# Passes outside, contraction tiles inside: a new order of the products in a split-precision block kernel

## The chip, the cores and the metric

One core of one Trainium2 chip. The metric is the device time of one execution in microseconds (us), the median of several.

## The reference

Two layers of a hybrid block on x, 1024 tokens by 1024 channels, float32. Each layer normalises x, projects it once into all branch inputs, runs four branches, gates and projects each, merges them by sigmoid gates, and adds one output projection to x.

```python
h = rms_norm(x, norm_g)
proj = h @ w_in
(q, k, v, z_a, p_in, z_b, u, v_sgu, z_c, glu_a, glu_b, z_d, merge) = jnp.split(proj, SPLIT_POINTS, axis=-1)
q = apply_rope(rms_norm(q...), cos, sin); k = apply_rope(rms_norm(k...), cos, sin)
o_a = window_attention(q, k, v, attn_sinks)
o_b = multiscale_pool(p_in, pool_mix, pool_scale)
o_c = spatial_gating(u, v_sgu, sgu_ln_g, sgu_ln_b, sgu_w, sgu_b)
o_d = conformer_conv(glu_a, glu_b, conv_w, conv_b, conv_ln_g, conv_ln_b)
...
return x + mixed @ w_out
```

## The kernel before

**Three passes.** TensorE multiplies in a rounded float32 format. To keep float32's precision, every operand is split into a rounded part ("hi": fhi, bhi, whi) and a rest (flo, blo, wlo), and a product is three matmuls, called passes here: hi by hi, lo of the data by hi of the weights, hi of the data by lo of the weights. ScalarE makes the rounded parts (a copy into the rounded format), GpSimd makes the rests of the weights (L718, a subtraction), VectorE the rests of the data (L1683, L1687).

**Stage pairs.** After the first two stages, each stage computes two tiles of 128 output channels by two halves of 512 tokens with seven products instead of eight (p1, p6, p5, p7, p2, p3, p4 in this order, a Winograd scheme): the operands are sums and differences of quarters of h (forms B11, B21, B22, B12, F5, F6, F7, F4) and of the weights (wsum). Each product has four tiles of contraction of 128 and three passes, 12 matmuls of 512 columns, written by the helper `three` (line L795). Its result goes to one of four PSUM banks a, b, c, d of `acc`; VectorE (sum_x, sum_v, sum_22, sum_12, sum_21) and ScalarE empty them. `three` runs the four tiles outside and the three passes inside, and the step begins when the rest of its weights is made (lo_made). There are four slots of split weights (SLOTS) and six of raw ones (RAWS).

**The beginning of a layer.** Stage VS (eight steps, L856 in layer 0, L885 in layer 1) has the tokens as output rows: data is the stationary operand, weights the moving one. In layer 0 the three passes are outside and four token tiles inside, and each part waits for its own hi or lo. Then `keys_values` (L906), four steps KV 0 to 3: keys and values also with tokens as rows, 256 columns (K and V side by side) for each of eight token tiles, eight contraction tiles and three passes. Slots F6 and F5 hold the first half of x until KV 1 is done, F7 and B21 the second half until KV 2 and 3. Then the stage pair Q 0 needs the forms of h: VectorE scales x by the norms (h_scale, using `spreads`, the reciprocal norms of all tokens broadcast to all partitions), forms F5, F7, F6, F4, ScalarE rounds them, VectorE subtracts for the rest. For B22, ScalarE copies the rounded part into PSUM (copy_b22), and VectorE subtracts from there (rest_b22); for the others it reads the rounded part from SBUF.

**Norms of layer 0.** ScalarE squares rows of x (row_squared, eight of them, spread over steps k = 1, 2, 3 by ROWS_AT), takes the root (rms_stage), waits for VectorE's reciprocal (norms) and stores the norms (store_norms), all at k = 3, ahead of x_rounded and the weights of k = 4. SP loads them back as `spreads`. SP's queue holds all loads of weights in order.

**Behind KV.** take_kv(0) and (1) on ScalarE copy K and V with the token's norm as scale (eight instructions each); turn_k, TensorE, turns K by eight transposes before p3 of Q 0; take_turned_k copies the result to kraw. square_a(0) and square_high(0) on ScalarE and square_low(0) on VectorE make the squares of K in two parts; head_sums(0) on TensorE (L960, L961) sums them before p5 of Q 1. inverse_root(0) on ScalarE follows. gate_stats, bn_aggr and a chain of small VectorE operations make the scaled gating values vsa; sgu_mix (L946), before p3 of Q 1, needs vsa and the root of K (qk_root).

All orders within an engine are written out by hand; engines meet at semaphores.

Of the kernel before, what the change touches and what calls it, by code (L numbers as in the profile page):

```python
# [6 lines left out]
F32 = mybir.dt.float32  # L7
# [140 lines left out]
def hybrid_block(nc, x, wstream, cols, rows, sgu_wt, pool_mix, rope, ident_in, edge_in, x_rows, out):  # L148
    ctx = ExitStack()
    with ctx:  # L150
# [80 lines left out]
        krow = place("krow", [P, TT, P], F32, at_t + 14336)  # L231
# [101 lines left out]
        b22_copied = sem("b22_copied")  # L333
        form_made = sem("form_made")
# [22 lines left out]
        kv_taken = sem("kv_taken")  # L357
        k_copied = sem("k_copied")
# [81 lines left out]

        def kv_bank(tile):

            return aux[:, tile // 4, tile % 4 * 2 * P:(tile % 4 + 1) * 2 * P]
# [341 lines left out]
        def _(pe):  # L785
            def three(dst, hi, lo, slot, kt0, first, last, cols=slice(0, HALF), resumed=False, half=None):


                for k in range(UK):
                    if half and k == UK // 2:  # L790
                        half()
                    wh = whi[:, slot, k * P:(k + 1) * P]
                    wl = wlo[:, slot, k * P:(k + 1) * P]
                    for n, (w, m) in enumerate(((wh, hi), (wh, lo), (wl, hi))):
                        mm = nc.tensor.matmul(dst, w, m[:, kt0 + k, cols], start=first and k == 0 and n == 0,  # L795
                                              stop=last and k == UK - 1 and n == 2, skip_group_check=resumed)
                return mm

            def pair(L, st, i, between=None):
                between = between or {}  # L800
                for q in PROD + (blocks(st, i) if st in MERGES else ()):
# [5 lines left out]
                    half = None  # L807
                    if (st, i) == ("Q", 0):
                        if q == "p1":
                            pe.wait_ge(form_ready, form_n(L, RESTS, "B22", 1))  # L810
                        pe.wait_ge(form_ready, form_n(L, RESTS, NEEDS[q], 0))

                        def half(q=q):
                            pe.wait_ge(form_ready, form_n(L, RESTS, NEEDS[q], 1))
                        pe.wait_ge(vs_taken, 8 * L + (6 if bank in "ab" else 8))
                    if (st, i) == ("O", 1) and q in ("p6", "p5", "p7", "p4"):
                        pe.wait_ge(mix_ready, mix_n(L, {"p6": "F6", "p5": "F5", "p7": "F7", "p4": "F4"}[q], 3))
                    pe.wait_ge(lo_made, split(L, st, i, name))
                    pe.wait_ge(taken[bank], bank_n(L, bank, (st, i), TAKEN_BEFORE[q]))
                    if (L, st, i, q) == (LAYERS - 1, "O", 3, "p4"):  # L820
# [3 lines left out]
                        for e in range(2):  # L824
                            at = slice(e * HALF // 2, (e + 1) * HALF // 2)
                            mm = three(BANK_AP["db"[e]][:, at], fhi[s], flo[s], slot, 0, e == 1, True, at,
                                       resumed=e == 0)
                            if e == 0:
                                mm.then_inc(end_done, 1)
                    elif q in PROD:  # L830
                        s = OPERAND[q]
                        mm = three(BANK_AP[bank], fhi[s], flo[s], slot, 0, q not in ("p2", "p4"), True,
                                   resumed=q in ("p2", "p4"), half=half)
                    else:
# [3 lines left out]
                        mm = three(BANK_AP[bank], bhi, blo, slot, 0, True, True, slice(t * HALF, (t + 1) * HALF))  # L838
# [53 lines left out]
            def keys_values(L):  # L892

                for k in range(4):
                    pe.wait_ge(lo_made, split(L, "KV", k))
                    slot = (L * FORMS + FORM["KV", k]) % SLOTS
                    for tile in range(TT):
                        if k == 0 and tile % 4 == 0:
                            pe.wait_ge(vs_taken, 8 * L + 2 + tile // 2)
                        for e in range(2):  # L900
                            kx = 2 * k + e
                            s = X_SLOT[kx // UK, tile // 4]
                            at = slice(tile % 4 * P, (tile % 4 + 1) * P)
                            w_at = slice(e * 2 * P, (e + 1) * 2 * P)
                            for m, (h, w) in enumerate(((fhi, whi), (flo, whi), (fhi, wlo))):
                                mm = nc.tensor.matmul(kv_bank(tile), h[s][:, kx % UK, at], w[:, slot, w_at],  # L906
                                                      start=kx == 0 and m == 0 and tile % 2 == 0,
# [202 lines left out]
        def _(act):  # L1110
# [339 lines left out]
            for k in range(1, KT):  # L1450
# [7 lines left out]
                for t in ROWS_AT[k]:  # L1458
                    row_squared(t)
# [1103 lines left out]
```

## Time and profile before

| | us |
|---|---|
| median of 3 runs (lowest, highest) | 2037.42 (2036.91, 2037.66) |
| the profiled execution | 2038.11 |
| its span, first to last instruction | 2036.2 |
| TensorE busy | 2031.4 |
| VectorE busy | 1347.7 |
| GpSimd busy | 1308.2 |
| ScalarE busy | 883.8 |

The granted clock of TensorE is 1.0 of full speed over the span. Busy time counts overlapping matmuls once; how long one takes is read from the distance of their starts, since each is shown with its own latency.

### The profile page before, as it was taken

How to read it: one execution, taken by the hardware profiler on the slowest of the kernel's cores; microseconds unless marked ns; L12 is line 12 of the kernel's file. 1: busy time of each engine (PE TensorE's matmuls, PEld its weight loads, DVE VectorE, ACT ScalarE, POOL GpSimd, SP SyncE). 2: the span in 40 equal slices, each digit the busy share in tenths (PEclk: the TensorE clock that was granted, in tenths of full speed). 3: DMA queues.
4: the chain of work that ended last, by engine and by line, in shares of the span. 5: the costliest groups of instructions: out<-in, count | busy, mean ns of one | idle time of the engine just before them, and what ended most of it. 6: DMA issues, size and time to landing. Idle time of an engine off the chain costs nothing.

```text
span 2036.2 us, 27175 instructions
## 1 busy us (share of the span) xinstructions
PE 2031.4 (100%) x9592; PEld 1690.7 (83%) x9592; DVE 1347.7 (66%) x1625; ACT 883.8 (43%) x1653; POOL 1308.2 (64%) x980
## 2 busy tenths in 40 slices
PE   9999999999999999999999999999999999999999
PEld 7988888888888888888888888888888888888887
DVE  5986543888878645338869764438888786453384
ACT  6655644343233334324647455443432343443242
POOL 2767555776669667554727675467766797675545
PEclk9999999999999999999999999999999999999999
DMA  7133323313431343313431332223135213434142
GB/s 277 38 94 86 93 92 112 96 52 84 90 72 52 83 83 79 138 52 114 145 90 37 104 94 94 99 89 94 57 78 97 65 57 81 91 73 145 42 135 104
DMA packets 122758, 186.13 MB, mean 91 GB/s; under 512 B 30976, under 2 KB 40320, under 8 KB 122624
## 3 DMA queue, kind: packets, MB, share of 16 engines
q1 hardware_dynamic: 105040, 155.14, 24.8%
q0 software_dynamic: 9216, 16.78, 6.1%
q10 hardware_dynamic: 8368, 12.47, 1.9%
q8 instruction: 78, 1.28, 0.3%
q14 instruction: 56, 0.46, 0.1%
HBM read 141.34 MB, written 41.95 MB: 90 GB/s over the span
## 4 chain that ended last, share of the span: by engine, by line
PE 97%; DVE 1%; DMA 1%; SPq 0%; ACT 0%; issue 0%; DVEq 0%; POOL 0%; ACTq 0%; POOLq 0%
PE acc L795 88%; PE aux L906 2%; PE acc L885 1%; PE aux L885 1%; PE aux L978 1%; PE acc L999 1%; PE aux L946 1%; PE aux L1014 1%; PE aux L986 1%; PE acc L856 1%; PE aux L856 1%; DVE flo L1683 0%; DMA x<-x 0%; DMA xrow<-x_rows 0%; PE aux L960 0%
## 5 line engine op out<-in xcount | busy, mean ns | idle before, releaser
L795 PE MATMUL acc<-fhi,whi 128*128 128x512 f32 x2140 | 834.9, 390 | 0.2 <-DVE x L1680 0.2
L718 POOL TENSOR_TENSOR wlo<-raw,whi 128x512 fp32r<-128x512 f32 x392 | 551.5, 1409 | 437.2 <-ACT whi L1112 436.4
L795 PE MATMUL acc<-fhi,wlo 128*128 128x512 f32 x2140 | 832.2, 389 | 0.0
L795 PE MATMUL acc<-flo,whi 128*128 128x512 f32 x2140 | 832.0, 389 | 0.0
L795 PEld LDWEIGHTS acc<-fhi,whi 128*128 128x128 f32 x2140 | 401.9, 188 | 83.6 <-issue 1.4
L795 PEld LDWEIGHTS acc<-fhi,wlo 128*128 128x128 f32 x2140 | 401.8, 188 | 83.5
L795 PEld LDWEIGHTS acc<-flo,whi 128*128 128x128 f32 x2140 | 401.9, 188 | 81.8
L718 POOL TENSOR_TENSOR wlo<-wsum,whi 128x512 fp32r<-128x512 f32 x222 | 320.6, 1444 | 195.4 <-ACT whi L1112 194.7
L1112 ACT ACTIVATE whi<-raw 128x512 fp32r<-128x512 f32 x392 | 245.7, 628 | 364.6 <-PE acc L795 321.1
L1687 DVE SCALAR_TENSOR_TENSOR aux<-conv,allp,aux 128x1024 f32<-128x1024 f32 x232 | 299.0, 1289 | 20.4 <-issue 0.9
L1112 ACT ACTIVATE whi<-wsum 128x512 fp32r<-128x512 f32 x222 | 139.8, 630 | 220.1 <-PE acc L795 164.3
L722 POOL TENSOR_TENSOR wsum<-wsum,raw 128x512 f32<-128x512 f32 x148 | 204.0, 1378 | 10.6
L795 PE MATMUL acc<-bhi,whi 128*128 128x512 f32 x512 | 200.4, 391 | 0.0
L795 PE MATMUL acc<-blo,whi 128*128 128x512 f32 x512 | 199.3, 389 | 0.0
L795 PE MATMUL acc<-bhi,wlo 128*128 128x512 f32 x512 | 199.3, 389 | 0.0
L1680 DVE TENSOR_TENSOR xs<-xs,acc 128x512 f32<-128x512 f32 x74 | 50.6, 684 | 130.6 <-PE acc L795 130.5
L722 POOL TENSOR_TENSOR wsum<-raw 128x512 f32<-128x512 f32 x74 | 98.3, 1328 | 39.4 <-ACT raw L1112 19.8
L795 PEld LDWEIGHTS acc<-bhi,whi 128*128 128x128 f32 x512 | 96.1, 188 | 21.2 <-issue 0.8
L795 PEld LDWEIGHTS acc<-bhi,wlo 128*128 128x128 f32 x512 | 96.1, 188 | 20.1
L795 PEld LDWEIGHTS acc<-blo,whi 128*128 128x128 f32 x512 | 96.2, 188 | 19.6
L722 POOL TENSOR_TENSOR raw<-raw 128x512 f32<-128x512 f32 x74 | 107.4, 1452 | 0.0
L1112 ACT ACTIVATE xs<-acc 128x512 f32<-128x512 f32 x74 | 44.3, 599 | 100.2 <-PE acc L795 100.2
(252 smaller groups left out, 2206.3 us busy)
## 6 DMA issues: line engine op xcount, KB each, us to landing
raw<-wstream SPq DMA_DIRECT2D x392, 256.0 KB, 2.8
md<-prev POOLq DMA_DIRECT2D x64, 256.0 KB, 4.3
x<-x SPq DMA_DIRECT2D x32, 256.0 KB, 4.8
md<-prev SPq DMA_DIRECT2D x32, 256.0 KB, 3.2
out<-x ACTq DMA_DIRECT2D x31, 256.0 KB, 2.1
mx<-md SPq DMA_DIRECT2D x24, 256.0 KB, 5.0
xrow<-x_rows SPq DMA_DIRECT2D x8, 512.0 KB, 6.7
qs<-qd SPq DMA_DIRECT2D x32, 128.0 KB, 2.8
```

Source lines behind the costliest of these rows:

```text
L718: nc.gpsimd.tensor_tensor(wlo[:, f % SLOTS, :], src, whi[:, f % SLOTS, :].bitcast(F32), ALU.subtract).then_inc(lo_made, 1)
L722: nc.gpsimd.tensor_tensor(out, a, b, ALU.add).then_inc(done, 1)
L795: mm = nc.tensor.matmul(dst, w, m[:, kt0 + k, cols], start=first and k == 0 and n == 0, stop=last and k == UK - 1 and n == 2, skip_group_c ...
L856: mm = nc.tensor.matmul(tile_bank(tile), h[s][:, k % UK, at], w[:, slot, :], start=k == 0 and m == 0, stop=k == KT - 1 and m == 2)
L885: mm = nc.tensor.matmul(tile_bank(tile), h[s][:, kx % UK, at], w[:, slot, :], start=kx == 0 and m == 0, stop=kx == KT - 1 and m == 2)
L906: mm = nc.tensor.matmul(kv_bank(tile), h[s][:, kx % UK, at], w[:, slot, w_at], start=kx == 0 and m == 0 and tile % 2 == 0, stop=kx == KT - ...
L946: mm = nc.tensor.matmul(aux[:, g % 2, n * P:(n + 1) * P], vs[g // 2][:, g % 2, n, :], sgt[:, g, :], start=True, stop=True)
L978: mm = nc.tensor.matmul(aux[:, m % 2, g * HALF + n * P:g * HALF + (n + 1) * P], qs[rows_g, m % 2, e, 2 * jp:2 * jp + 2, :], keys, start=Tr ...
L986: mm = nc.tensor.transpose(aux[:, m % 2, n * P:(n + 1) * P], prob[m % 2][:, n, :], ident[:])
L1112: return nc.scalar.activation(dst, src, ACT.Copy)
L1680: return nc.vector.tensor_tensor(out, a, b, ALU.add)
L1687: return nc.vector.scalar_tensor_tensor(out=out, in0=a, scalar=s, in1=b, op0=ALU.mult, op1=op)
```

## The change

1. In `three` the passes are outside and the four contraction tiles inside: hi by hi, then data hi by weights lo, then data lo by weights hi. A step now begins when the rounded weights are there (hi_made); before the second pass it waits for the weights' rest (lo_made), and in Q 0 and O 1, before tiles 0 and 2 of the third pass, for the data's rests.
2. `keys_values` has the channels as output rows: the weights are stationary (128 by 128), the data moves, 512 tokens at a time; K is in aux[:, 0, :], V in aux[:, 1, :]. V is copied by ScalarE (copy_v), turned by TensorE before p7 of Q 0 (turn_v), and copied back with the norms as scale (take_v). K needs no turning: VectorE multiplies it by the spread norms (scale_k).
3. The rest of F6 is made as that of B22 is: ScalarE copies the rounded part into PSUM (copy_f6), VectorE subtracts from there (rest_f6). p1 of Q 0 waits for F6's second rest, as these copies lie in its banks.
4. In layer 0, the last two rows of squares, the root and the store of the norms go from k = 3 to k = 4, VectorE's reciprocal from before k = 4 to before k = 5.
5. In Q 0 VectorE's order is sum_22, rests of F4, scale_k, five tiles of gate_stats, sum_12, instead of two tiles, sum_22, rests of F4, three tiles, sum_12.

```diff
-                for k in range(UK):
-                    if half and k == UK // 2:
-                        half()
-                    wh = whi[:, slot, k * P:(k + 1) * P]
-                    wl = wlo[:, slot, k * P:(k + 1) * P]
-                    for n, (w, m) in enumerate(((wh, hi), (wh, lo), (wl, hi))):
...
+                for n, (w, m) in enumerate(((whi, hi), (wlo, hi), (whi, lo))):
+                    if n == 1 and low:
+                        low()
+                    for k in range(UK):
+                        if n == 2 and rest and k % 2 == 0:
+                            rest(k // 2)
+                        mm = nc.tensor.matmul(dst, w[:, slot, k * P:(k + 1) * P], m[:, kt0 + k, cols],
...
+                    def low(name=name):
+                        pe.wait_ge(lo_made, split(L, st, i, name))
...
                         if q == "p1":
-                            pe.wait_ge(form_ready, form_n(L, RESTS, "B22", 1))
-                        pe.wait_ge(form_ready, form_n(L, RESTS, NEEDS[q], 0))
+                            pe.wait_ge(form_ready, form_n(L, RESTS, "F6", 1))
+                        pe.wait_ge(form_hi, form_n(L, HIGHS, NEEDS[q], 1))
...
-                    pe.wait_ge(lo_made, split(L, st, i, name))
+                    pe.wait_ge(hi_made, split(L, st, i, name))
...
+                    for kx in (2 * k, 2 * k + 1):
+                        for c in range(2):
...
+                            for t in range(2):
+                                s = X_SLOT[kx // UK, t]
+                                for m, (w, h) in enumerate(((wh, fhi), (wh, flo), (wl, fhi))):
+                                    mm = nc.tensor.matmul(aux[:, c, t * HALF:(t + 1) * HALF], w, h[s][:, kx % UK, :],
...
-                pair(L, "Q", 0, {"p3": lambda L=L: turn_k(L), "p4": lambda L=L: row_sums(L)})
+                pair(L, "Q", 0, {"p7": lambda L=L: turn_v(L), "p4": lambda L=L: row_sums(L)})
...
+            def copy_f6(L, n):
+
+                act.wait_ge(form_hi, form_n(L, HIGHS, "F6", n))
+                act.wait_ge(form_ready, form_n(L, RESTS, "B22", n))
+                copy(acc[:, 1 - n, :], fhi[S_F6][:, 2 * n:2 * n + 2, :].rearrange("p k t -> p (k t)").bitcast(F32)
+                     ).then_inc(f6_copied, 1)
...
-                for t in ROWS_AT[k]:
+                for t in ROWS_AT[k] if k < 3 else ROWS_AT[3] if k == 4 else ():
                     row_squared(t)
-                if k == 3:
+                if k == 4:
                     rms_stage(0)
                     store_norms(0)
...
+            def scale_k(L):
+                dve.wait_ge(step_done, stepped(L, "KV", 3))
+                mul(kraw[:], aux[:, 0, :], spreads[:]).then_inc(k_scaled, 1)
...
-                if k == 4:
+                if k == 5:
                     norms(0)
...
-                form_rest(L, ("F6", 0), ("F6", 1), ("F5", 0), ("F5", 1))
+                rest_f6(L)
+                form_rest(L, ("F5", 0), ("F5", 1))
...
-                dve.wait_ge(vs_taken, 8 * L + 8)
-                gate_stats(range(2))
                 sum_22(L, "Q", 0, qhi[0][:, HALF:SEQ])
                 form_rest(L, ("F4", 0), ("F4", 1))
-                gate_stats(range(2, 5))
+                scale_k(L)
+                dve.wait_ge(vs_taken, 8 * L + 8)
+                gate_stats(range(5))
```

## Rows read from the trace of the kernel before

**Rows 1.** The page, busy time of each engine, its share, instructions.
```profile
PE 2031.4 (100%) x9592; PEld 1690.7 (83%) x9592; DVE 1347.7 (66%) x1625; ACT 883.8 (43%) x1653; POOL 1308.2 (64%) x980
```
**Rows 2.** Chain that ended last, whole span: start us, us, what.
```profile
38.12 2.72 PE acc L856 x12
...
51.72 23.03 PE aux L906 x192
...
750.34 212.19 PE acc L795 x936
...
1123.46 3.57 PE aux L946 x32
```
**Rows 3.** Waits of TensorE: us in total, times, longest.
```profile
PE acc L795 <- DVE x L1680: 0.2, 1, 0.2
```
**Rows 4.** TensorE's timeline at 27 to 31: start us, us, what.
```profile
27.51 1.07 PE L856 MATMUL acc<-whi,flo 128*128 128x512 f32 x4
29.08 1.21 PE L856 MATMUL aux<-whi,fhi 128*128 128x512 f32 x4 [0.50 <-ACT whi L1112]
30.55 1.19 PE L856 MATMUL aux<-wlo,fhi 128*128 128x512 f32 x4 [0.26 <-POOL wlo L718]
```
**Rows 5.** ScalarE's timeline at 25 to 29, its DMA issues too.
```profile
25.03 1.06 ACT L1156 ACTIVATE xrow<-xrow 128x1024 f32<-128x1024 f32 x1
...
26.21 0.30 ACT L1164 ACTIVATE rms<-rms,epst 128x8 f32<-128x8 f32 x1
26.77 0.35 ACTq L1170 DMA_DIRECT2D rd<-rms  x1
27.17 1.34 ACT L1184 ACTIVATE fhi<-x,allp 128x512 fp32r<-128x512 f32 x2 [0.66 <-DVE rms L1700]
28.42 0.61 ACT L1112 ACTIVATE whi<-raw 128x512 fp32r<-128x512 f32 x1
```
**Rows 6.** Tile x, its two transfers issued between 18 and 19.
```profile
DMA to landing us min/median/max: 5.8/6.8/7.8
```
**Rows 7.** GpSimd's timeline at 29, the rest of weights 4.
```profile
29.17 1.33 POOL L718 TENSOR_TENSOR wlo<-raw,whi 128x512 fp32r<-128x512 f32 x1 [5.50 <-ACT whi L1112]
```
**Rows 8.** VectorE's timeline, layer 0, 29 to 109.
```profile
29.68 7.93 DVE L1687 SCALAR_TENSOR_TENSOR flo<-x,allp,fhi 128x512 fp32r<-128x512 f32 x6 [0.33 <-ACT fhi L1184]
...
39.61 11.18 DVE L1687 SCALAR_TENSOR_TENSOR x<-x,allp,spreads 128x512 f32<-128x512 f32 x12
...
62.61 2.34 DVE L1683 TENSOR_TENSOR flo<-x,acc 128x1024 fp32r<-128x1024 f32 x2
65.05 3.54 DVE L1687 SCALAR_TENSOR_TENSOR x<-x,x 128x1024 f32<-128x1024 f32 x2
68.51 12.60 DVE L1683 TENSOR_TENSOR flo<-x,fhi 128x1024 fp32r<-128x1024 f32 x8
...
96.38 1.80 DVE L1683 TENSOR_TENSOR tmpr<-tmp,sqh 128x1024 fp32r<-128x1024 f32 x1
...
105.45 2.67 DVE L2109 TENSOR_SCALAR vsa<-vsa,rstd,shift 128x256 f32<-128x256 f32 x8
```
**Rows 9.** DMA issues at 31 to 32: KB each, us to landing.
```profile
spreads<-rd SPq DMA_DIRECT2D x1, 512.0 KB, 4.6
```
**Rows 10.** ScalarE's timeline, layer 0, 50 to 118.
```profile
55.99 1.03 ACT L1112 ACTIVATE acc<-fhi 128x1024 f32<-128x1024 f32 x1
...
107.17 1.03 ACT L1387 ACTIVATE tmp<-aux 128x1024 f32<-128x1024 f32 x1
```
**Rows 11.** Chain that ended last, 80 to 130.
```profile
100.64 0.24 PE aux L960
...
109.74 3.57 PE aux L946 x32
```
**Rows 12.** VectorE's timeline, layer 1, rest of K's squares.
```profile
1109.63 1.22 DVE L1683 TENSOR_TENSOR tmpr<-tmp,sqh 128x1024 fp32r<-128x1024 f32 x1
```
**Rows 13.** ScalarE's timeline, layer 1, root of K.
```profile
1119.11 1.02 ACT L1387 ACTIVATE tmp<-aux 128x1024 f32<-128x1024 f32 x1
```

More of the change, by code:

```diff
@@ L785, in _, with three @@
         def _(pe):
-            def three(dst, hi, lo, slot, kt0, first, last, cols=slice(0, HALF), resumed=False, half=None):
-                for k in range(UK):
-                    if half and k == UK // 2:
-                        half()
-                    wh = whi[:, slot, k * P:(k + 1) * P]
-                    wl = wlo[:, slot, k * P:(k + 1) * P]
-                    for n, (w, m) in enumerate(((wh, hi), (wh, lo), (wl, hi))):
-                        mm = nc.tensor.matmul(dst, w, m[:, kt0 + k, cols], start=first and k == 0 and n == 0,
-                                              stop=last and k == UK - 1 and n == 2, skip_group_check=resumed)
+            def three(dst, hi, lo, slot, kt0, first, last, cols=slice(0, HALF), resumed=False, low=None, rest=None):
+                for n, (w, m) in enumerate(((whi, hi), (wlo, hi), (whi, lo))):
[5 more added lines that the diff above has]
+                        mm = nc.tensor.matmul(dst, w[:, slot, k * P:(k + 1) * P], m[:, kt0 + k, cols],
+                                              start=first and k == 0 and n == 0, stop=last and k == UK - 1 and n == 2,
+                                              skip_group_check=resumed)
                 return mm
@@ L832, in pair @@
                         mm = three(BANK_AP[bank], fhi[s], flo[s], slot, 0, q not in ("p2", "p4"), True,
-                                   resumed=q in ("p2", "p4"), half=half)
+                                   resumed=q in ("p2", "p4"), low=low, rest=rest)
                     else:
@@ L1358, in square_a @@
                 else:
-                    act.wait_ge(k_copied, L + 1)
+                    act.wait_ge(k_scaled, L + 1)
                 if n == 2:
@@ L1497, in _ @@
                 next_high(L, "KV", 1)
-                form_rounded(L, ("F6", 0), ("F6", 1), ("F5", 0), ("F5", 1))
+                for n in range(2):
+                    form_rounded(L, ("F6", n))
+                    copy_f6(L, n)
+                form_rounded(L, ("F5", 0), ("F5", 1))
                 next_high(L, "KV", 2)
@@ L1721, in rest_b22, with rest_f6 @@
                         acc[:, 1 - n, :]).then_inc(form_ready, 1)
+            def rest_f6(L):
+                for n in range(2):
+                    at = slice(2 * n, 2 * n + 2)
+                    dve.wait_ge(f6_copied, 2 * L + n + 1)
+                    sub(flo[S_F6][:, at, :].rearrange("p k t -> p (k t)"), x22[:, at, :].rearrange("p k t -> p (k t)"),
+                        acc[:, 1 - n, :]).then_inc(form_ready, 1)
             def form(L, q):
```

73 lines of the change are left out of this document (35 added, 38 removed).

## The prediction

> **What bounds the kernel now.** I read the page first, for the engines' shares: TensorE is busy 2031.4 us of a span of 2036.2 us [rows 1]. So nothing that another engine saves shortens the kernel. Time comes only from fewer or shorter matmuls, or from a gap of TensorE that closes, and is lost only where a new gap opens. The chain that ended last gives the pitch of the matmuls: 936 products of 512 columns in 212.19 us, 226.7 ns each, and 192 of 256 columns in 23.03 us, 119.9 ns each [rows 2]. A product thus costs its columns at 2.4 GHz (213.3 and 106.7 ns) and 13.3 ns more, and the reader should keep that 13.3.
>
> Then the gaps. The waits of TensorE name one from a bank that VectorE had not emptied, 0.2 us, late in layer 0 [rows 3]; the new order waits for that bank as the old one does, so it stays. The other gap is at the start, in TensorE's timeline [rows 4]: four products begin every 0.91 us there (4 by 0.2267), but from 27.51 to 29.08 it is 1.57 us and from there to 30.55 it is 1.47 us, together 1.22 us too much.
>
> **Edit 1, keys and values with channels as output rows.** 192 products of 256 columns become 96 of 512 in each layer. By the rows, 96 x 0.2267 = 21.76 us against 23.03: 1.27 us less a layer, 2.5 us in both [rows 2]. All of it is on TensorE's path. The Trainium skill, "TensorE: Matmul & The Clock Gate", section "Back-to-back issue gap", has N / 2.4 + 2.5 ns for a product; by that, an estimate, the saving would be 192 x 109.2 - 96 x 215.8 = 0.25 us a layer. The rows have 13.3 ns where the page has 2.5, and the rows decide. Turning V instead of K is again eight transposes of the same shape, only earlier in the same pair, so it costs what it cost.
>
> **Edit 2, the three passes outside.** Of the 7,956 products at L795 none is added or taken away. Before, two neighbours often share the weights; now each has its own. Does that cost? The trace has both forms: L856 runs the passes outside (each product with new weights) and takes 2.72 us for 12, L795 runs them inside and takes 212.19 / 936 x 12 = 2.72 us [rows 2]. So nothing. What it buys is that the rests of weights and operands may come one or two thirds of a product later (0.9 and 1.8 us), and since nearly no gap of the steady stages waits for a rest, it buys nothing there. The added waits for rests stand in TensorE's queue alone; behind them stand the next products, and L856 shows waits between its passes that cost nothing where they are met. If the cover were gone, each would cost what the rest is late.
>
> **Edit 3, the norms one step later in layer 0.** ScalarE's timeline [rows 5]: between weights 3 and 4 it squares two rows and takes the root (26.21) before it may round x of step 4 at 27.17, and weights 4 come at 28.42; TensorE wanted them at 28.42 and got them at 29.03. Now x of step 4 goes first. Its transfer, issued at 18.6 at the latest, lands within 7.8 us [rows 6], at 26.4; rounding (1.25, from 27.17 to 28.42) and weights (0.61) end at 28.2, in time, and their rest, 1.33 us on GpSimd [rows 7], at 29.6, some 0.2 us after its pass. So about 1.0 us of the 1.22 is got back. Who is late next? Everything behind the norms on ScalarE: two rows (1.2 each, 25.03 to 26.21) and from the root to the next rounding 0.96 make 3.4 us, so step 5 begins at 26.4 + 1.85 + 3.4 = 31.65 where it began right behind weights 4, at 29.0. TensorE wants step 5 at 28.42 + 6 x 0.907 = 33.9, so it does not feel it. But VectorE's rests of steps 5 to 7 hang on those roundings. They ran 29.68 to 37.6 [rows 8]. Now the first can start at 32.4 and the last two, with two more steps of 1.85 and a rounding ahead, not before 36.7. Two rests alone are 1.4 us (end 38.1), all six at the old pace 7.93 us (end 40.3): 0.5 to 2.7 us later. I take 1.8, nearer the old pace, because GpSimd works at the same times as before. The store of the norms moves from 27.0 to some 31.4 too, and SP's queue (the spread norms, then the weights of keys and values, wanted only past 50) waits for it. Scaling would start at 39.61 + 1.8 = 41.4, and the load of the spread norms took 4.6 us [rows 9], which leaves the store 5.4 us: VectorE's rests and memsets cover it.
>
> This matters since VectorE has no idle time from 39.61, where it starts to scale h, to past 101 in layer 0. What it is late at 39.61 it is late at the end.
>
> **Edit 4, F6 through PSUM and K scaled on VectorE.** The rest of F6 now needs two copies by ScalarE, 1.03 us each [rows 10]. F6's second half is formed at 65.05 + 3.54 = 68.6 [rows 8]. Before, both rests were done at 68.51 + 2 x 1.21 = 70.9 (1.21, as 1.22 in [rows 12], is such a rest that meets nobody). Now follow a rounding and a copy of the same length, 1.03 each, and a rest from PSUM of 1.17 (62.61, 2.34 for two): 71.8, and with the hand-overs 71.9, so 1.0 us late. The eight rests from SBUF took 12.60 us, so collisions with GpSimd are in these prices as they were. The product of K with the norms is one more VectorE instruction of 1024 columns from PSUM, 1.17 us by the same row, ahead of everything that the head sums need. ScalarE loses eight scalings of K and a copy and gains three copies, about even, and it is not what is last. VectorE's new order in Q 0 has the same five tiles of gate_stats ahead of the squares' rest as the old one, so it moves no gate: 0. Only F4's rests come earlier.
>
> **The sum, layer 0.** TensorE without gaps would reach the head sums at 100.64 - 1.27 - 1.0 = 98.4 [rows 11]. They wait for the rest of K's squares, which ended at 96.38 + 1.80 = 98.2 [rows 8] and now ends at 98.2 + 1.8 + 1.0 + 1.2 = 102.2. So they begin at 102.2 and not 100.64: the 2.3 us are gone and 1.6 us more. The next gate is the gating mix at 109.74, which wants the scaled values (105.45 + 2.67 = 108.1) and K's root from ScalarE (107.17 + 1.03 = 108.2) [rows 8, 10, 11]: 108.2 + 4.0 = 112.2 against 109.74 + 1.6 = 111.3. If VectorE meets GpSimd less there it is less. Layer 0 in all: between +1.6 and +2.5, I take +2.0.
>
> **The sum, layer 1.** There edit 3 does not act, and VectorE waits for the spread norms anyway. The same two gates ended at 1109.63 + 1.22 = 1110.85 and 1119.11 + 1.02 = 1120.1 [rows 12, 13], the mix began at 1123.46 [rows 2]. Later by 2.2 they are at 1113.05 and 1122.3, TensorE, whose layer 1 lies 1123.46 - 109.74 = 1013.72 us behind layer 0, wants them at 100.64 + 1013.72 - 1.27 = 1113.1 and at 1123.46 - 1.27 = 1122.2. They just fit, so this layer keeps about 1.3 us: -1.3. Unmet, it keeps nothing.
>
> Together +2.0 - 1.3 = +0.7 us. The profiled execution took 2038.11 us, 1.9 more than its span, and lies 0.7 above the median of the three runs, so on the median: 2037.42 + 0.7 = 2038.1 us.
>
> **The rivals.**
> *The gates have slack enough.* If VectorE's rests of steps 5 to 7 end only 0.5 us late and it meets GpSimd less, the wait in layer 0 shrinks to nothing, and all of edits 1 and 3 remains: -2.5 - 1.0 = -3.5, 2033.9 us. For it: GpSimd has pauses, and eight rests took 12.60 us where 8 x 1.21 would be 9.7 [rows 8], so 2.9 us of collisions could fall out. Against it: the same work on both engines has to meet again. Half way to it is likelier than the whole.
> *VectorE's debt is bigger than TensorE's gain in both layers.* Place: head sums and mix; price: each us of further delay is one us of the kernel in layer 0, and in layer 1 after the first 0.1. With 2.7 for 1.8 and 1 us of further collisions in each layer: +0.7 + 1.9 + 1.0, and more if the store takes over 5.4 us: 2041 to 2042. As worked out, the change loses once layer 0 costs more than the 1.3 us that layer 1 saves, and leaves the band of no change once this debt exceeds 3.4 us more than forecast.
> *The pitch moves.* One ns on 7,956 products is 8 us. The rows of L856 and L795 speak against it at some 0.1 ns; I leave it 6 in 100 over both sides.
>
> **How the numbers follow.** Forecast and its neighbourhood (2036 to 2040) 0.60; slack enough, wholly or half, 0.24; debt in both layers 0.10; pitch 0.06. What a measurement can tell from no change is 0.2%, 4.1 us: faster means under 2033.3, slower over 2041.5. The full gain, 2033.9, stops just short of the first; with the pitch and luck 0.07 lie beyond it. Beyond the other lies half of the big debt and half of the pitch, 0.10. The rest, 0.83, is the same. The range 2034.6 to 2040.6 leaves out the whole gain and the big debt.
>
> **What would show it.** Right: 96 products in 21.8 us at the keys and values; no gap over 0.3 us between 27 and 31; VectorE's scaling of h begins near 41.4, the head sums of layer 0 begin near 102 after a gap released by VectorE's rest of the squares, and those of layer 1 begin with none. Wrong: head sums under 100 in layer 0 (slack), gaps in layer 1, twelve products in anything but 2.72 us, or a gap at any other product of Q 0, such as at its first, for F6's second rest, which I have a little ahead of it.

## The result and the profile after

The changed kernel takes 2041.46 us (median of 20 runs, 2039.15 to 2043.07), the kernel before 2037.48 (20 runs beside them, 2036.53 to 2039.05): a ratio of 1.0020, 95% interval 1.0014 to 1.0026. It is 4.0 us slower where +0.7 was forecast, and outside the range. The profiled execution took 2041.62 us with a span of 2039.8, 3.6 more than before; this is the sum that the traces have to explain.

The page, busy time of each engine after the change:

```profile
PE 2031.1 (100%) x9400; PEld 1681.2 (82%) x9400; DVE 1356.1 (66%) x1627; ACT 883.7 (43%) x1641; POOL 1314.6 (64%) x980
```

TensorE was to lose 2.5 us of busy time with 192 products fewer than in [rows 1], and lost 0.3. Busy time counts a product by how long it takes, so something runs slower. Its waits (us in total, times, longest) answer to [rows 3]:

```profile
PE acc L793 <- DVE flo L1700: 2.9, 1, 2.9
PE acc L1062 <- DVE st L2055: 1.1, 1, 1.1
PE acc L793 <- DVE v L1697: 0.7, 1, 0.7
PE aux L967 <- DVE tmpr L1700: 0.6, 2, 0.4
PE aux L864 <- ACT fhi L1191: 0.4, 1, 0.4
PE acc L793 <- DVE x L1697: 0.2, 1, 0.2
```

The waits at L1062 and for x are there before too in like size. The 0.4 us at L864 stand at 6.41, ahead of everything that the change touches in that stage; other profiled kernels show between 0 and 0.8 us there, so it belongs to the execution. The two waits of [rows 4], at 29.08 and 30.55, are gone. New are the first, for F6's rest, the third, for the bank that VectorE empties in sum_v, and the fourth, the head sums. The first stands here in TensorE's timeline of layer 0:

```profile
72.28 0.39 PE L914 MATMUL aux<-fhi,wlo 128*128 128x512 f32 x1
75.58 1.20 PE L793 MATMUL acc<-fhi,whi 128*128 128x512 f32 x4 [2.92 <-DVE flo L1700]
76.62 1.58 PE L793 MATMUL acc<-fhi,wlo 128*128 128x512 f32 x4
78.00 1.91 PE L793 MATMUL acc<-flo,whi 128*128 128x512 f32 x4
79.70 1.41 PE L793 MATMUL acc<-fhi,whi 128*128 128x512 f32 x4
80.95 1.07 PE L793 MATMUL acc<-fhi,wlo 128*128 128x512 f32 x4
...
92.72 0.47 PE L793 MATMUL acc<-fhi,whi 128*128 128x512 f32 x1 [0.74 <-DVE v L1697]
...
104.71 0.50 PE L967 MATMUL aux<-sqh,heads_r 128*128 128x512 f32 x1 [0.38 <-DVE tmpr L1700]
```

Read the starts. Four products should take 0.91 us; the groups at 76.62, 78.00 and 79.70 take 1.38, 1.70 and 1.25, some 1.6 us too much together, although nothing is waited for. The busy time by stretch (its length; TensorE, its weight loads, VectorE, ScalarE, GpSimd; the granted clock, DMA share and GB/s) says why:

```profile
70.00:76.00 6.00, 3.08 (x14) 2.25 (x13) 4.17 (x5) 5.82 (x6) 0.00 (x0) 1.00 0.00 0
76.00:81.00 5.00, 5.00 (x17) 3.92 (x16) 5.00 (x4) 5.00 (x8) 3.93 (x2) 0.66 0.18 53
81.00:90.00 9.00, 9.00 (x45) 7.54 (x44) 8.82 (x5) 4.16 (x7) 9.00 (x5) 1.00 0.11 31
```

The clock was 0.66 from 76 to 81 and 1.00 on both sides: seven products stand 427 ns apart, which is 512 columns at 1.2 GHz, and the one on either side of them is slow in part. They follow a stretch in which TensorE stood still for 3 us.

VectorE's timeline, the counterpart of [rows 8]:

```profile
33.83 5.49 DVE L1704 SCALAR_TENSOR_TENSOR flo<-x,allp,fhi 128x512 fp32r<-128x512 f32 x4 [0.33 <-ACT fhi L1191]
...
41.34 11.18 DVE L1704 SCALAR_TENSOR_TENSOR x<-x,allp,spreads 128x512 f32<-128x512 f32 x12
...
66.36 2.34 DVE L1700 TENSOR_TENSOR flo<-x,acc 128x1024 fp32r<-128x1024 f32 x2
68.80 2.54 DVE L1704 SCALAR_TENSOR_TENSOR x<-x,x 128x1024 f32<-128x1024 f32 x2
72.27 1.22 DVE L1700 TENSOR_TENSOR flo<-x,acc 128x1024 fp32r<-128x1024 f32 x1 [0.93 <-ACT acc L1119]
74.31 1.22 DVE L1700 TENSOR_TENSOR flo<-x,acc 128x1024 fp32r<-128x1024 f32 x1 [0.81 <-ACT acc L1119]
75.44 11.28 DVE L1700 TENSOR_TENSOR flo<-x,fhi 128x1024 fp32r<-128x1024 f32 x6
...
97.02 1.21 DVE L1694 TENSOR_TENSOR kraw<-aux,spreads 128x1024 f32<-128x1024 f32 x1
...
102.96 1.69 DVE L1700 TENSOR_TENSOR tmpr<-tmp,sqh 128x1024 fp32r<-128x1024 f32 x1
```

Except for the two waits for ScalarE's copies, VectorE never waits for another engine here from 41.34 to the end of the squares' rest at 104.65; the head sums begin 0.06 us after it. That end was 98.18 before: 6.5 us later, where I had worked out 4.0.

ScalarE's timeline of the two F6 copies:

```profile
70.12 1.06 ACT L1119 ACTIVATE fhi<-x 128x1024 fp32r<-128x1024 f32 x1 [6.54 <-DVE x L1704]
71.21 1.03 ACT L1119 ACTIVATE acc<-fhi 128x1024 f32<-128x1024 f32 x1
72.17 1.04 ACT L1119 ACTIVATE fhi<-x 128x1024 fp32r<-128x1024 f32 x1
73.25 1.03 ACT L1119 ACTIVATE acc<-fhi 128x1024 f32<-128x1024 f32 x1
```

Round, copy, round, copy in series: the second copy ends at 74.28, though the second half of F6 was formed at 71.34.

The chain that ended last gives the stages as in [rows 2, 11]:

```profile
114.10 3.57 PE aux L953 x32
...
754.74 212.19 PE acc L793 x936
...
1069.89 21.76 PE aux L914 x96
...
1127.06 3.57 PE aux L953 x32
```

The ledger goes by the starts in TensorE's timeline. The kernel before has its head sums there at 100.47; the 100.64 of [rows 11] is the same product in the chain, whose piece begins where the product before it ends:

```profile
100.47 0.41 PE L960 MATMUL aux<-sqh,heads_r 128*128 128x512 f32 x1
```

Keys and values begin at 50.75 and not at 51.56, -0.8; they take 21.76 us, -1.3; the gap ahead of p1 (72.51 to 75.58) +3.1; the slower clock +1.6; the gap ahead of p3 +0.9; the one ahead of the head sums +0.5; the first products behind the gaps, which start a little slower, +0.2. That is +4.2 at the head sums, which begin at 104.71 for 100.47, and +4.4 at the mix, 114.10 for 109.74. Layer 1, from mix to mix, is 1012.96 us for 1013.72: -0.8. Together +3.6, the whole span.

### The profile page after: what moved, and what is told of

The parts are those of the page before. It is cut to its first block, busy times and chain, and to the rows that moved or that the text cites. A ratio compares the mean times of both kernels' runs of the same rounds, so it can differ in the third digit from the quotient of the medians.

```text
span 2039.8 us, 26783 instructions
## 1 busy us (share of the span) xinstructions
PE 2031.1 (100%) x9400; PEld 1681.2 (82%) x9400; DVE 1356.1 (66%) x1627; ACT 883.7 (43%) x1641; POOL 1314.6 (64%) x980
## 3 DMA queue, kind: packets, MB, share of 16 engines
q8 instruction: 76, 1.25, 0.3%
## 4 chain that ended last, share of the span: by engine, by line
PE 94%; DVE 3%; DMA 1%; DVEq 1%; ACT 0%; SPq 0%; issue 0%; ACTq 0%
PE acc L793 87%; PE acc L893 1%; PE aux L893 1%; PE aux L914 1%; PE aux L985 1%; PE acc L1006 1%; PE aux L953 1%; PE aux L1021 1%; PE aux L993 1%; DVE x L1704 1%; DVE flo L1700 1%; DVE x L1700 0%; DMA xrow<-x_rows 0%; DMA raw<-wstream 0%; DVE stv L2103 0%; DVE flo L1704 0%
## 5 line engine op out<-in xcount | busy, mean ns | idle before, releaser
L793 PE MATMUL acc<-fhi,whi 128*128 128x512 f32 x2140 | 575.0, 390 | 3.9 <-DVE flo L1700 2.9
L793 PE MATMUL acc<-flo,whi 128*128 128x512 f32 x2140 | 572.1, 389 | 0.0
L793 PE MATMUL acc<-fhi,wlo 128*128 128x512 f32 x2140 | 571.7, 389 | 0.0
L793 PE MATMUL acc<-bhi,whi 128*128 128x512 f32 x512 | 138.1, 391 | 0.0
L793 PE MATMUL acc<-bhi,wlo 128*128 128x512 f32 x512 | 136.9, 389 | 0.0
L793 PE MATMUL acc<-blo,whi 128*128 128x512 f32 x512 | 136.8, 389 | 0.0
```

Of the source, the lines that this page charges most:

```text
L793: mm = nc.tensor.matmul(dst, w[:, slot, k * P:(k + 1) * P], m[:, kt0 + k, cols], start=first and k == 0 and n == 0, stop=last and k == UK ...
```

## The experiments

Each kernel ran 5 rounds beside the kernel before, whose medians in the three batches were 2037.34, 2037.23 and 2037.45 us. "Squares" is the end of VectorE's rest of K's squares in layer 0, "heads" the start of the head sums, "scaling" the start of VectorE's scaling of h, all read from the one profiled execution of each. The ratios lie nearer to the means than to the medians: e2's mean is 2.2 us above that of the kernel before, its median 2.8.

| kernel | us (range, runs) | ratio (95%) | scaling | squares | heads |
|---|---|---|---|---|---|
| before | 2037.48 | 1 | 39.61 | 98.18 | 100.47 |
| after | 2041.46 | 1.0020 (1.0014-1.0026) | 41.34 | 104.65 | 104.71 |
| e1 | 2038.79 (2038.13-2040.59, 11) | 1.0008 (0.9998-1.0017) | 38.35 | 100.79 | 100.84 |
| e2 | 2040.14 (2037.28-2041.8, 11) | 1.0010 (1.0001-1.0019) | 40.86 | 102.35 | 103.52 |
| e3 | 2036.36 (2035.44-2037.52, 11) | 0.9995 (0.9986-1.0004) | 38.52 | 99.22 | 99.27 |
| e4 | 2043.29 (2041.14-2044.29, 7) | 1.0027 (1.0017-1.0038) | 41.04 | 104.27 | 105.45 |
| e5 | 2040.92 (2038.96-2041.98, 11) | 1.0015 (1.0007-1.0024) | 40.84 | 101.37 | 103.61 |
| e6 | 2037.37 (2036.07-2037.92, 11) | 1.0000 (0.9991-1.0009) | 39.03 | 97.61 | 99.86 |
| e7 | 2036.38 (2035.37-2037.48, 11) | 0.9996 (0.9988-1.0005) | 38.64 | 98.09 | 98.89 |
| e8 | 2042.55 (2040.87-2043.51, 7) | 1.0026 (1.0015-1.0036) | 39.92 | 102.58 | 102.64 |
| e9 | 2035.88 (2035.07-2036.58, 11) | 0.9992 (0.9984-1.0001) | 37.58 | 99.14 | 99.19 |
| e10 | 2036.68 (2035.54-2037.35, 11) | 0.9996 (0.9987-1.0005) | 39.77 | 100.41 | 100.46 |
| e11 | 2037.33 (2036.62-2038.1, 11) | 0.9999 (0.9990-1.0008) | 36.32 | 95.93 | 99.06 |
| e12 | 2040.52 (2038.3-2040.95, 11) | 1.0014 (1.0005-1.0023) | 40.71 | 102.22 | 103.02 |

**e1, edit 3 undone.**

```diff
-                for t in ROWS_AT[k] if k < 3 else ROWS_AT[3] if k == 4 else ():
+                for t in ROWS_AT[k]:
...
-                if k == 4:
+                if k == 3:
                     rms_stage(0)
...
-                if k == 5:
+                if k == 4:
                     norms(0)
```

> The changed kernel with edit 3 undone (norms of layer 0 at k = 3 and before k = 4 again). Theory A, VectorE's chain in layer 0 is what TensorE waits for: scaling of h begins near 39.6 and not 41.34, all that follows on VectorE is 1.7 us earlier, the gap at the first product of Q 0 shrinks from 3.1 to about 0.6 us, and the kernel takes 1.7 to 2.7 us less, about 2039. Rival B, the order of the passes with its waits costs time everywhere: the time stays at 2041 within 0.5 us. Rival C, the gap of 3.1 us and the clock's fall behind it are the price by themselves: 2.5 us of gap and 1.6 us of clock less, about 2037.3.

Against the changed kernel 2.7 us come back. In the profiled execution the gap ahead of p1 is gone and the granted clock stays 1.00 throughout the stretch; p3 waits 1.8 us for sum_v, and 0.7 us in layer 1, where the changed kernel's profile shows no such wait.

**e2, F6's rests from SBUF again**, edit 3 kept; p1 waits for B22 again.

```diff
-                for n in range(2):
-                    form_rounded(L, ("F6", n))
-                    copy_f6(L, n)
-                form_rounded(L, ("F5", 0), ("F5", 1))
+                form_rounded(L, ("F6", 0), ("F6", 1), ("F5", 0), ("F5", 1))
...
-                rest_f6(L)
-                form_rest(L, ("F5", 0), ("F5", 1))
+                form_rest(L, ("F6", 0), ("F6", 1), ("F5", 0), ("F5", 1))
```

> The changed kernel with F6's rests made from SBUF as before, without ScalarE's copies into PSUM; the first product of Q 0 then waits for B22 alone. Theory A: VectorE's chain is 1.6 us shorter, the gap at the first product is gone, but a gap of some 3 to 4 us opens at p3 of Q 0, which waits for sum_v; the kernel takes about 1.7 us less, 2039.7. Rival C (the gap at p1 and the clock behind it are the price): 3.1 + 1.6 less, 2036.8. Rival B: no change.

The wait at p1 is gone; the debt shows up at p3. TensorE's timeline of e2:

```profile
85.64 1.07 PE L793 MATMUL acc<-flo,whi 128*128 128x512 f32 x4
90.45 1.32 PE L793 MATMUL acc<-fhi,whi 128*128 128x512 f32 x4 [3.74 <-DVE v L1694]
91.57 1.91 PE L793 MATMUL acc<-fhi,wlo 128*128 128x512 f32 x4
93.28 1.75 PE L793 MATMUL acc<-flo,whi 128*128 128x512 f32 x4
```

A gap of 4 us, and behind it again seven products 427 ns apart. This time the fall lies behind VectorE's gate at p3, not ahead of it, and the head sums begin 1.17 us after the squares' rest: TensorE itself is late. Not every execution of e2 is like this one. The mean granted clock of each is known to three places: three of the 11 kept 1.000 and took 2037.28 to 2037.62 us, the eight below 1.000 took 2039.03 to 2041.8.

**e3, both undone.** The edits of e1 and e2 together: keys and values, the passes, scale_k and the new order in Q 0 stay.

> Edits 3 and F6's way both undone: passes outside, keys and values with channels as rows, K scaled on VectorE remain. Theory A: VectorE's chain 3.4 us earlier, head sums of layer 0 near 101.3, gating mix near 110.5, layer 1 keeps 1.3: 2037 to 2037.9, no worse than before. Rival B: still 2 us or more above the kernel before.

1.0 us under the kernel before, better than expected, though the interval of the ratio includes 1. Edit 1's 2.5 us are thus kept in part: the head sums still wait for the squares in both layers, and layer 1, mix to mix, is 0.6 us shorter than before. Edit 1 and scale_k were not run by themselves. With e1, e2 and the changed kernel this makes a square: neither 2036.36, F6's copies alone 2038.79 (+2.4), the later norms alone 2040.14 (+3.8), both 2041.46 (+5.1).

**e4, the two PSUM banks of F6's copies exchanged**, so that p1 needs the first of the rests only.

```diff
-                        if q == "p1":
-                            pe.wait_ge(form_ready, form_n(L, RESTS, "F6", 1))
+                        if q == "p1":
+                            pe.wait_ge(form_ready, form_n(L, RESTS, "F6", 0))
...
-                copy(acc[:, 1 - n, :], fhi[S_F6]...
+                copy(acc[:, n, :], fhi[S_F6]...
```

> The changed kernel with the two PSUM copies of F6 in each other's banks, so that p1 and p6 of Q 0 need only F6's first rest, ready 2 us earlier. Nothing in VectorE's chain changes. Theory A: the gap at p1 shrinks by 2 us to 1.1 and the clock may not fall, but what is won comes back as a longer wait of p3 for sum_v and of the head sums, so the kernel's time stays within 0.5 us of 2041. Rival C: 2 us of gap and 1.6 us of clock less, 2037.9.

A miss: it was expected within 0.5 us of 2041. The wait at p1 falls from 2.9 to 0.9 us, VectorE's squares end 0.4 earlier, and the kernel is 1.8 us slower than the changed one. The 4.1 us that it now waits at p3 bring the clock's fall behind that gate, where nothing covers it: the head sums come 1.18 us after the squares. By the profiles that is 0.6 us at the mix of layer 0; 1.0 us more comes in layer 1, where p3 waits 0.7 us.

**e5, edit 3 alone on the kernel before.**

```diff
-                for t in ROWS_AT[k]:
+                for t in ROWS_AT[k] if k < 3 else ROWS_AT[3] if k == 4 else ():
...
-                if k == 3:
+                if k == 4:
                     rms_stage(0)
...
-                if k == 4:
+                if k == 5:
                     norms(0)
```

> The kernel before with edit 3 alone. Theory A: TensorE's gap of 1.2 us near 28 is gone but VectorE's chain is 1.7 us late at its start and some 2.7 us late by F6, so a gap opens at p3 of Q 0 (sum_v) and at the gating mix of layer 0, and the kernel takes about 1.2 us more, 2038.6. Rival, the gap closed at 28 is kept: 1 us less, 2036.4.

Edit 3 costs 3.7 us by itself (3.2 by the means), three times what was expected; p3 waits as expected. TensorE's timeline of e5 shows one of its slow products after another, 0.43 us apart:

```profile
90.56 0.47 PE L795 MATMUL acc<-fhi,whi 128*128 128x512 f32 x1 [2.57 <-DVE v L1680]
...
92.49 0.63 PE L795 MATMUL acc<-flo,whi 128*128 128x512 f32 x1
92.92 0.63 PE L795 MATMUL acc<-fhi,wlo 128*128 128x512 f32 x1
```

and the granted clock by stretch in e5:

```profile
89.00:92.20 3.20, 1.64 (x7) 1.37 (x8) 3.03 (x8) 2.57 (x4) 3.06 (x3) 0.96 0.46 160
92.20:95.60 3.40, 3.40 (x10) 2.69 (x9) 3.40 (x3) 1.03 (x2) 3.40 (x3) 0.54 0.00 0
95.60:100.00 4.40, 4.40 (x21) 3.60 (x21) 4.23 (x10) 3.16 (x4) 2.71 (x2) 1.00 0.00 0
```

The clock falls some 1.4 us after the work has resumed, not in the gap.

**e6, edit 2 alone on the kernel before** (the new `three` and its waits, everything else as before).

> The kernel before with edit 2 alone (passes outside, tiles inside, waits for rests at their passes). Theory A: no gap of the steady stages waited for a rest, the pitch stays 226.7 ns, so 2037.4 within 0.4 us. Rival B, the order or its waits cost: above 2038.

No change within 0.1%. Twelve products cost the same in the new order.

**e7, as e3, with three instead of five tiles of gate_stats ahead of the squares' rest.**

```diff
-                gate_stats(range(5))
+                gate_stats(range(3))
...
-                gate_stats(range(5, TT))
+                gate_stats(range(3, TT))
```

> Edits 3 and F6's way undone, and VectorE makes the rest of K's squares after three tiles of gate_stats instead of five, 1.3 us earlier. Theory A: the head sums' gaps of 0.5 us in layer 0 and 0.4 us in layer 1 close, the next gate (scaled gating values) does not move, so up to 0.9 us less than with the five tiles: 2035.6. If the scaled values or K's root bind the gating mix next, nothing is won: 2036.4.

The wait at the head sums is gone; the mix now waits 0.6 us for ScalarE's root (about 0.3 in each layer), and p3 0.4 us in layer 0. Nothing is won: 2036.38 against e3's 2036.36.

**e8, both roundings of F6 ahead of both copies.**

```diff
-                for n in range(2):
-                    form_rounded(L, ("F6", n))
-                    copy_f6(L, n)
+                form_rounded(L, ("F6", 0), ("F6", 1))
+                copy_f6(L, 0)
+                copy_f6(L, 1)
```

> The changed kernel, but ScalarE rounds both halves of F6 before it copies either into PSUM. Theory A: F6's second rest is ready 0.8 us earlier, if that part of the price is ScalarE's serial order, and VectorE's chain with it; the gap at p1 is 2.3 us instead of 3.1 and the kernel takes 0.8 us less, 2040.5. If the clock no longer falls behind the shorter gap, that adds nothing, since p3 then waits longer for sum_v. Rival C: the missing fall of the clock is worth its 1.6 us, 2039.

A miss. VectorE's timeline of e8:

```profile
71.10 2.35 DVE L1700 TENSOR_TENSOR flo<-x,acc 128x1024 fp32r<-128x1024 f32 x2 [2.10 <-ACT acc L1119]
```

The rests now follow each other, but VectorE waits 2.1 us in one piece where it waited 0.9 and 0.8. F6 is done 4.5 us after it was formed (68.99 to 73.45); in the changed kernel it was 4.2 us, and 2.3 before. The profile's layer 0 is 2.1 us shorter (its mix begins at 112.00), of which 1.4 come from the scaling's earlier start, which this edit does not touch; its layer 1 is 2.1 us longer than the changed kernel's, with a wait of 1.7 us at p3, and the median 1.1 longer.

**e9, as e3, with VectorE's small constants early.** In layer 0 the two signs, the sinks' negatives and the blocks of ones are made behind the rests of step 2, where VectorE waits anyway, instead of just ahead of the scaling of h.

```diff
                 for t in (1, 0):
                     x_rest(0, k, t)
+                if k == 2:
+                    dve.wait_ge(cols_loaded, 16)
+                    ...
+                    nc.vector.tensor_scalar(nsink[:], allp[:, 0, C_SINK:C_SINK + 8], -1.0, None, ALU.mult)
+                    blocks_of_ones()
```

> Edits 3 and F6's way undone, and VectorE's block of small constants of layer 0 (1.8 us between its rests of x and its scaling of h) moved into its idle time behind step 2. Theory A: scaling of h begins 1.5 us earlier, the gaps at p3 (0.2 us) and at the head sums of layer 0 (0.5 us) close: 0.7 us less than without, 2035.7, under both kernels. If the gap at the head sums has another cause: 2036.4.

The shortest median of all, 1.6 us under the kernel before, though the interval (0.9984 to 1.0001) just touches 1, and only 0.5 under e3. The squares end hardly earlier (99.14 for 99.22): the start's gain is lost again on the way.

**e10, as e2 with the same constants early; e11, the kernel before with them.**

> The changed kernel with F6 made as before and the same constants early; edit 3 (norms one step later) is kept. Theory A: VectorE's chain starts 1.5 us earlier than in the kernel with F6 back alone (2040.1), the gap at p3 of Q 0 in layer 0 falls from 3.9 to 2.4 us, and the clock does not fall behind a gap of that length (2.2 and 2.7 us did not let it): 1.5 us of chain and up to 1.3 us of clock less, 2037.3 to 2038.6. Rival (edit 3 costs in another way than through VectorE's late start): 2040.

> The kernel before with the same constants early. Theory A: before the change no gap of TensorE hung on VectorE's chain, so 1.5 us on VectorE are worth nothing: 2037.3 within 0.4 us.

e10 is 3.5 us faster than e2, more than was expected, for 1.1 us of earlier scaling: the squares come 1.9 us sooner, the wait at p3 is 1.3 for 3.7, and the clock does not fall, so most of the 1.17 between squares and heads is gone as well. 1.9 + 1.1 are the 3.06 us by which the heads are earlier. e11 starts the scaling 3.3 us earlier than the kernel before (moving the constants is worth 1.8, the rest differs from execution to execution) and gains nothing: in the kernel before, no gate of this stretch waited for VectorE.

**e12, the gap at p3 filled.** From e2; V is turned ahead of p3 instead of p7, ScalarE copies it back later to match, and in layer 0 14 products whose result is overwritten run first, so TensorE is not idle.

```diff
                 pe.wait_ge(v_copied, L + 1)
+                if L == 0:
+                    for _ in range(14):
+                        nc.tensor.matmul(aux[:, 1, 0:HALF], ones_r[:], fhi[S_B22][:, 0, :], start=True, stop=True)
```

> The changed kernel with F6 made as before, V turned at p3 instead of p7, and in layer 0 fourteen products of 512 columns (3.2 us) ahead of the turning, into the bank that the turning overwrites: TensorE works through most of the gap of 4 us in which it waits for sum_v. p3 cannot start earlier by it. Theory A with the clock as a price of its own: the clock does not fall to 1.2 GHz behind the gap, the 1.6 us of slow products go, and as the head sums then wait 0.3 us more for VectorE, the kernel takes 1.3 us less than with F6 back alone, 2038.8. If the clock's fall has another cause, or was hidden by later waits: 2040.1, unchanged.

TensorE's timeline of e12:

```profile
85.60 3.37 PE L941 MATMUL aux<-fhi,ones_r 128*128 128x512 f32 x14
88.81 1.04 PE L943 MATMUL aux<-ident,vraw 128*128 128x128 f32 x8
90.31 1.16 PE L793 MATMUL acc<-fhi,whi 128*128 128x512 f32 x4 [0.47 <-DVE v L1697]
91.31 1.08 PE L793 MATMUL acc<-fhi,wlo 128*128 128x512 f32 x4
92.23 1.07 PE L793 MATMUL acc<-flo,whi 128*128 128x512 f32 x4
94.30 0.47 PE L931 MATMUL aux<-srow,ones_r 128*128 128x512 f32 x1 [1.00 <-ACT vt L1366]
```

p3 begins when it did in e2 (90.31 for 90.45), and its twelve products are done 1.7 us sooner, without slow ones. All 11 executions kept a mean granted clock of 1.000, where eight of e2's 11 did not. So it was the idle time and not the late gate that brought the clock's fall. The gain does not reach the end: turning V so late makes the row sums wait 1.0 us for ScalarE in each layer. The median, 2040.52, is not distinct from e2's and is the time expected if nothing were won, so this run does not show that keeping the clock wins time. It also lies 3 us above the three executions of e2 that kept the clock; those were not profiled, so why they are that fast is open.

## Why the prediction was wrong

**The step that failed is the size of VectorE's debt at the squares' rest: 1.8 + 1.0 + 1.2 = 4.0 us forecast, 6.5 measured.** The mechanism and the place where it ends stood in the forecast; two earlier gates did not. Split by start of the scaling and the stretch from there to the squares (98.18 - 39.61 = 58.6 before, 63.3 after):

| term | forecast | measured |
|---|---|---|
| scaling begins later | 1.8 | 1.7 (41.34 for 39.61) |
| F6 through PSUM | 1.0 | 1.8 (stretch: after 63.3, e2 61.5; e1 62.4, e3 60.7) |
| scale_k, with keys and values and the new order | 1.2 | 2.1 (e3 60.7, before 58.6) |
| other meetings with GpSimd, since all is later | 0 | 0.8 (e2 61.5, e3 60.7) |
| sum | 4.0 | 6.4 |

Each measured term is a difference of two single executions, and the start of the scaling varies: among the kernels that leave the constants in place it lies between 38.35 and 39.61 without edit 3 (five, mean 38.8) and between 39.92 and 41.34 with it (six, mean 40.8). The kernel before is the latest of its group and the changed one of its own. So edit 3 makes VectorE late by about 2.0 us, and that the forecast's 41.4 was hit to 0.1 is partly luck.

*F6.* I let one rounding, one copy and one rest follow the forming of the second half. But ScalarE was still rounding and copying the first half then (70.12 to 72.24), since the two halves are formed 1.27 us apart and take ScalarE 2.1 each. The two waits of VectorE, 0.93 and 0.81, are that, and F6 takes 4.2 us from formed to done (71.34 to 75.53) where 3.3 were reckoned. In e8's order they still take 4.5.

*Meetings with GpSimd.* I took it that "collisions with GpSimd are in these prices as they were". They were not. VectorE and GpSimd in the kernel before:

```profile
53.16 2.54 DVE L1683 TENSOR_TENSOR x<-x,x 128x1024 f32<-128x1024 f32 x2
...
55.15 1.70 POOL L718 TENSOR_TENSOR wlo<-raw,whi 128x512 fp32r<-128x512 f32 x1 [6.23 <-ACT whi L1112]
```

and the same two operations after the change:

```profile
54.88 4.39 DVE L1700 TENSOR_TENSOR x<-x,x 128x1024 f32<-128x1024 f32 x2
...
54.34 1.61 POOL L716 TENSOR_TENSOR wlo<-raw,whi 128x512 fp32r<-128x512 f32 x1 [4.36 <-ACT whi L1119]
55.91 2.28 POOL L736 TENSOR_TENSOR srow<-sgt,srow 128x512 fp32r<-128x512 f32 x1
```

Before, the pair fell almost wholly into a pause of GpSimd and took 2.54 us; 1.7 us later it falls beside GpSimd and takes 4.39, 1.85 more. F6's forming, 2.54 for 3.54 [rows 8], gives 1.0 back, now that it lies in a pause. The same two changes stand between e3 and e2, and their net is the last term. The eight rests took 12.60 us before and 13.72 in e3, 1.1 more, which with scale_k's 1.21 accounts for the third term. In e5, where VectorE has the instructions of before, the stretch grew from 58.6 to 60.5 with its later start; in e11 it grew to 59.6 with an earlier one. It depends on where the operations meet GpSimd, and not on lateness as such.

**Edit 3's gain.** The forecast gave it 1.0 us of the 1.22 in [rows 4], and took these for the kernel's. They were that execution's. e1 has the norms at k = 3 as the kernel before, and loses nothing at the same place:

```profile
28.88 1.07 PE L864 MATMUL aux<-whi,fhi 128*128 128x512 f32 x4
29.78 1.07 PE L864 MATMUL aux<-wlo,fhi 128*128 128x512 f32 x4
```

Keys and values begin between 50.14 and 51.56 in the seven profiled kernels without edit 3 (mean 50.8, the kernel before the latest), and between 50.24 and 50.80 in the seven with it (mean 50.5). So the gain is nearer to 0.4 us than to 1.0, and the 0.8 of the ledger is a difference of two executions.

**The gates that I did not count.** I named Q 0's first product as a place that would prove me wrong, "for F6's second rest, which I have a little ahead of it". It was 2.9 us behind. And p3's wait for sum_v stood nowhere in the forecast, though it was the tighter gate: sum_v ended at 86.97 before and p3 began at 89.01, a slack of 2.0 us, of which TensorE's own gain ahead of it (0.8 + 1.3) leaves nothing. By the forecast's own 2.8 us of debt at that place, p3 would have waited that long. In layer 0 of the changed kernel the gap at p1, the slow clock and the gap at p3 are together 5.6 us, and sum_v ends 5.6 later than before (92.57): they are one debt, met in three portions. From p3 to the head sums TensorE needs 11.5 us (89.01 to 100.47), so 92.72 + 11.5 = 104.2, and the last 0.5 is the squares' own gate. The head sums start 0.05 or 0.06 us behind the squares in the changed kernel, e1, e3, e8, e9 and e10 alike, wherever the gaps ahead of them stand. 104.65 for the forecast 102.2 is 2.45 of the 2.9 us missed in the span; the rest is layer 1.

**The clock.** Not in the forecast at all. Behind a long gap some eight products run at 1.2 GHz, which costs 1.6 us. In the changed kernel that is covered, as TensorE waits for VectorE twice more after it (0.74 and 0.38 us); VectorE, with no idle time, does not feel it. In e2, e4 and e5 it lies behind p3's gate, and there 1.2, 1.2 and 2.2 us lie between squares and heads. So e4 is slower than the changed kernel in layer 0 with less debt. In e5 the way from p3 to the head sums takes 13.05 us for 11.46: 1.6 of the 3.1 us lost there is the clock's, the other 1.6 p3's later start (90.56 for 89.01).

**Layer 1** was forecast at -1.3 with gates that just fit. It is -0.8. The squares end 2.4 us later than before, taken from the mix (1117.63 - 1110.85 - 4.36), where 2.2 were reckoned; the forecast had 0.1 to spare, and with 100.47 for 100.64 it would have lacked 0.1. A wait opens at the head sums. The -0.8 is not firm either: e1 has the same instructions in layer 1 and takes 1014.11 us from mix to mix, 1.2 more.

**What held.** Keys and values 21.76 us; the pitch of the matmuls, 212.19 us for 936, to the last digit, and e6 without effect; no gap between 27 and 31, though not by edit 3 alone; scaling near 41.4 (41.34); the head sums behind a gap released by VectorE, later than "near 102". Edit 3 is a net loss by every pair: 3.7 us alone (e5), 3.8 without F6's copies (e2 against e3), 2.7 with them (the changed kernel against e1). The trade was visible in the forecast, a gain of 1.0 against a debt of 1.8; the gain is smaller, and the debt meets gates that were not counted.

**The rivals.** "VectorE's debt is bigger than TensorE's gain in both layers" gave 2041 to 2042 and is what came, by further collisions as it said, except that layer 1 kept a part; it had 0.10. "Gates have slack enough" fell: e11 shows that there was slack, e5 that it was less than the 3.2 to 3.4 us by which edit 3 alone makes squares and sum_v late. "The pitch moves" fell with e6.

**Open.** The mean granted clock lies below 1.000 in 11 of 20 executions of the changed kernel, 5 of 11 of e1, 8 of 11 of e2, 7 of 7 of e4, 3 of 11 of e5 and 4 of 7 of e8, and in none of e3, e6, e7, e9 to e12 or of the 91 of the kernel before that ran beside the experiments. Where a kernel has both kinds, those below 1.000 took 0.9 to 2.9 us more in the mean (2042.0 for 2040.8 in the changed kernel, 2040.4 for 2037.5 in e2). So the clock is part of the spread, 3.9 us in the changed kernel and 4.5 in e2 for 2.5 in the kernel before. But 2.9 is more than the 1.6 that one fall costs in the traces, and a longer wait would bring both the fall and a longer time: how much is whose is open, as only one execution of each kernel was profiled.

## What to carry to other kernels

Before moving work to or ahead of an engine that has no idle time until the next gate, list every gate behind that engine with its slack (here 2.0 us at p3 and 2.3 at the head sums, less what TensorE itself gains), and compare each with the sum of all delays up to it, collisions included: within the slack a delay is free, beyond it it costs in full. An edit that saves TensorE less than 1 us at one place can lose 3 us net two stages later if it starts the other engine's long chain later. Before pricing a small gap from one profile, look for it in a second execution: the gap at 28 was not in e1's. And a gap of TensorE of some 3 us may cost more than its length, so one long gap is worse than the same time in small ones, unless a later wait covers it.

## What the runs showed of the hardware

**The clock behind a gap.** In the profiled executions seven or eight products 427 ns apart followed waits of 2.57 (e5), 2.92 (changed), 3.74 (e2) and 4.07 us (e4), and none followed waits of 1.26 (e10), 1.82 (e1) and 2.36 us (e8), or e12, where other products filled the gap. The length of the wait does not settle it alone: other executions of e1 and e8 had a mean granted clock below 1.000, and some of e2 and e5 had not. The clock falls 0.8 to 1.4 us after the work has resumed. The Trainium skill, "TensorE: Matmul & The Clock Gate", section "What's actually happening", has the clock follow how busy the array has been recently; the traces agree: the fall came behind idle time at p1 or at p3, and not where the idle time was filled.

**Two operands in SBUF while GpSimd works.** The six rests from 75.44 take 1.88 us on average, but not evenly: the first, while GpSimd stands still, and the second, which it joins, take 1.22 each, and the last four, with GpSimd at work, 2.31 each. With one operand in PSUM it makes no difference: over the 14 traces, 50 such subtractions of 128x1024 had GpSimd at work beside them from start to end, and each took 1.21 us, as the one at 66.36. The Trainium skill, "SBUF — State Buffer", section "SBUF: two separate sides", calls the port that both share an exclusive lock for an operation of VectorE with two SBUF inputs; the rows agree. In layer 0 the way through PSUM saved nothing on the two rests of F6: GpSimd stood still from 70 to 76, and before the change the two took 1.21 and 1.23 from SBUF. It only added the two copies of 1.03 us ahead of them.
